# Another hand-written order of the attention phase on three engines of a two-block transformer kernel

## The chip, the cores and the metric

The kernel runs on one core of one Trainium2 chip. The metric is the device time of one execution in microseconds, lower is better. Of the kernel before there are three timed executions: 1290.80, 1287.97 and 1290.04 us, median 1290.04.

## The reference

256 rows of 1024 values pass through two layers of a first block and one layer of a second block, all in fp32. A layer of the first block, which the change touches, is:

```
h = rms_norm(x, attn_norm_g); z = h @ w_in
q, k of three kinds: rms_norm per head of 64, rotary tables
moba: 4 heads, causal softmax, values of 64
diff: 4 heads, softmax(q1 k1) - lam * softmax(q2 k2), values of 128, rms_norm, gain
dsa:  an indexer (8 heads: relu(q k), weighted sum) keeps the 64 best causal keys per row;
      4 heads attend to these alone
x = x + concat(moba, diff, dsa) @ w_out
h2 = rms_norm(x, ffn_norm_g)
x = x + (silu(h2 @ w_gate) * (h2 @ w_up)) @ w_down
```

## The kernel before, in words

The 256 rows are two row blocks r = 0, 1 of 128. Every large product is three matmuls: each fp32 operand is split into a high part and a low part, and high by high, high by low and low by high are summed in PSUM (lines 587 to 589). Weights come by DMA from SP's queue in chunks of 1 MB into a ring of three slots `raw`. ACT writes a chunk's high part (`split_hi`, in the attention phase called `hi(p, j)`, line 1227), DVE subtracts to get the low part (`split_lo`, `lo(p, j)`, line 1684), PE multiplies. ACT may write a slot's high part only when PE has used the chunk three before it; SP may load a slot when DVE is done with it.

Each engine (PE = TensorE, ACT = ScalarE, DVE = VectorE, POOL = GpSimd, SP = SyncE) runs its own program in the order in which it is written, and waits on semaphores. For the attention phase of each of the two layers the orders on PE, ACT and DVE are three long lists of calls, written out by hand; both layers use the same lists. Their parts are:

- `row_product(p, j, r)` on PE: product p (0 to 7, columns of `w_in`), half j of the depth, row block r. `copy_z(l, p, r)` on ACT moves the result from PSUM to `z`. (Below, a product half is one such call.)
- `square_heads`, `head_sums`, `scale_heads(l, s)`: ACT, DVE and ACT again form the per-head norm of head set s, 0 to 3. POOL rotates and scales the set (lines 510 to 522) and takes the norm from `scale_heads`. POOL works through the index heads first (line 517 ends them), then through the sets MQ, DQ, DK, SQ.
- `turn_heads(s, b)` on PE transposes a finished set (here s = 0 index heads, 1 index key, 2 MQ, 3 DQ, 4 DK, 5 SQ), `heads_copy` on ACT copies it to `headsT`. `index_key` on DVE rotates the index key.
- `index_scores`, `index_relu`, `index_sum`, `topk_rounds`, `topk_mask`: the indexer, on PE, ACT and DVE.
- For four groups of heads g = 0 to 3 (moba, diff, dsa, diff): `group_scores` on PE, `attend_mask` on DVE, `attend_exp` on ACT, for the diff groups `blend` on DVE (line 1865), `group_turn` on PE, `attend_copy` or `blend_copy` on ACT and DVE, `group_values` on PE; then `attend_out` on DVE, or `diff_stats` on ACT and `diff_norm` on DVE (lines 1885, 1890). All groups share the PSUM banks 2 to 4 for scores and bank 5 for values.
- `mix_turn` on PE turns the mixed rows, `turned_hi_copy` and `turned_lo_copy` split them, `out_product(n, j, r)` multiplies by `w_out`.
- POOL also subtracts for the chunks 18 and 20 of each layer (line 548); DVE passes these on by `lo_from_pool`.

Two waits tie the groups together and are quoted, for the scores and for the values:

```python
def attend_scores(A, q, k):
    eng.wait_ge(pT_act, 2 * A + 2)
    eng.wait_ge(pT_dve, A + 1)
...
def attend_values(A, v, dv):
    eng.wait_ge(pT_act, 2 * A + 4)
    eng.wait_ge(pT_dve, A + 2)
    eng.wait_ge(o_done, A + 2)
```

`A` counts groups over both layers. A group's scores thus wait until the turned probabilities of the group before are copied, and its values until the result of the group before has left bank 5.

## Time and profile before

| | |
|---|---|
| time, median of three | 1290.04 us |
| profiled execution, its own time | 1290.8 us |
| its span in the trace | 1289.0 us |
| PE busy | 1256.7 us, 97% |
| DVE busy | 823.2 us, 64% |
| ACT busy | 662.2 us, 51% |
| POOL busy | 184.3 us, 14% |
| chain that ended last | PE 82%, DVE 9%, issue 4%, ACT 3% |

The span is what the trace covers, the time also holds what lies around it. A busy share is an average over the whole program. In the chain of waits each moment of the span is put down to the engine that was waited for. The attention phase of layer 0 runs from 24 to 162 us of the span, that of layer 1 from 359 to 493 us. An idle time in brackets behind a row of the timeline is what the engine stood still just before the row, and what ended it.

### The profile page before, as it was taken

How to read it: one execution, taken by the hardware profiler on the slowest of the kernel's cores; microseconds unless marked ns; L12 is line 12 of the kernel's file. 1: busy time of each engine (PE TensorE's matmuls, PEld its weight loads, DVE VectorE, ACT ScalarE, POOL GpSimd, SP SyncE). 2: the span in 40 equal slices, each digit the busy share in tenths (PEclk: the TensorE clock that was granted, in tenths of full speed). 3: DMA queues.
4: the chain of work that ended last, by engine and by line, in shares of the span. 5: the costliest groups of instructions: out<-in, count | busy, mean ns of one | idle time of the engine just before them, and what ended most of it. 6: DMA issues, size and time to landing. Idle time of an engine off the chain costs nothing.

```text
span 1289.0 us, 16912 instructions
## 1 busy us (share of the span) xinstructions
PE 1256.7 (97%) x6430; PEld 1059.2 (82%) x6430; DVE 823.2 (64%) x983; ACT 662.2 (51%) x981; POOL 184.3 (14%) x162
## 2 busy tenths in 40 slices
PE   8999999999999999999999999999999999999998
PEld 6779788888887978888888899788997777888886
DVE  5898664455669876554457655866695676655444
ACT  5567454434564756344435544644547654634443
POOL 5863200000177620000000000000000003000000
PEclk9989999999999999999999998999999999999999
DMA  7424355556462434555564563343334355455551
GB/s 263 183 74 144 131 196 196 184 179 219 139 209 75 160 135 146 213 191 195 180 220 157 205 215 112 122 146 102 127 107 173 148 191 189 169 186 193 195 198 46
DMA packets 34219, 213.12 MB, mean 165 GB/s; under 512 B 4305, under 2 KB 5585, under 8 KB 11506
## 3 DMA queue, kind: packets, MB, share of 16 engines
q1 hardware_dynamic: 34098, 212.21, 46.6%
q8 instruction: 38, 0.62, 0.2%
q14 instruction: 19, 0.16, 0.0%
q0 software_dynamic: 64, 0.13, 0.0%
HBM read 211.28 MB, written 1.05 MB: 165 GB/s over the span
## 4 chain that ended last, share of the span: by engine, by line
PE 82%; DVE 9%; issue 4%; ACT 3%; DMA 1%; POOL 1%; POOLq 0%; DVEq 0%; ACTq 0%
PE bank L587 23%; PE bank L589 22%; PE bank L588 22%; PE bank L1001 3%; DVE wlo L1684 2%; PE bank L694 2%; PE bank L753 2%; ACT whi L1227 1%; DVE index L1778 1%; PE bank L841 1%; PE bank L713 1%; DMA raw<-in_w_values 1%; PE bank L615 1%; DVE z L2163 1%; PE bank L1111 1%
## 5 line engine op out<-in xcount | busy, mean ns | idle before, releaser
L1684 DVE TENSOR_TENSOR wlo<-raw,whi 128x2048 fp32r<-128x2048 f32 (+4 forms) x197 | 439.3, 2234 | 252.1 <-ACT whi L1227 250.6
L1227 ACT ACTIVATE whi<-raw 128x2048 fp32r<-128x2048 f32 (+5 forms) x201 | 369.3, 1843 | 133.9 <-PE bank L589 125.7
L587 PE MATMUL bank<-whi,hT_hi 128*128 128x512 f32 (+4 forms) x1040 | 408.2, 393 | 6.7 <-DVE wlo L1684 3.4
L589 PE MATMUL bank<-whi,hT_lo 128*128 128x512 f32 (+4 forms) x1040 | 399.4, 384 | 0.0
L588 PE MATMUL bank<-wlo,hT_hi 128*128 128x512 f32 (+4 forms) x1040 | 398.8, 383 | 0.0
L587 PEld LDWEIGHTS bank<-whi,hT_hi 128*128 128x128 f32 x1040 | 197.4, 190 | 46.7 <-issue 7.2
L589 PEld LDWEIGHTS bank<-whi,hT_lo 128*128 128x128 f32 x1040 | 196.9, 189 | 36.6
L588 PEld LDWEIGHTS bank<-wlo,hT_hi 128*128 128x128 f32 x1040 | 197.6, 190 | 33.3
L587 PE MATMUL bank<-whi,mixT_hi 128*128 128x512 f32 (+1 forms) x248 | 96.4, 389 | 6.5 <-DVE mixT_lo L1719 3.7
L589 PE MATMUL bank<-whi,mixT_lo 128*128 128x512 f32 (+1 forms) x248 | 94.5, 381 | 0.0
L588 PE MATMUL bank<-wlo,mixT_hi 128*128 128x512 f32 (+1 forms) x248 | 94.2, 380 | 0.0
L587 PE MATMUL bank<-whi,ffT_hi 128*128 128x512 f32 x240 | 93.7, 390 | 0.0
L589 PE MATMUL bank<-whi,ffT_lo 128*128 128x512 f32 x240 | 93.5, 390 | 0.0
L588 PE MATMUL bank<-wlo,ffT_hi 128*128 128x512 f32 x240 | 93.4, 389 | 0.0
L1350 ACT ACTIVATE sqr<-bank,ssq 128x256 f32<-128x256 f32 x66 | 31.1, 473 | 88.0 <-PE bank L589 88.0
L1359 ACT ACTIVATE ffT_hi<-bank 128x256 fp32r<-128x256 f32 x60 | 19.8, 382 | 101.1 <-PE bank L841 101.1
L587 PEld LDWEIGHTS bank<-whi,mixT_hi 128*128 128x128 f32 (+1 forms) x248 | 47.2, 190 | 16.5 <-issue 3.4
L1915 DVE SCALAR_TENSOR_TENSOR probs<-bank,ssq,sqr 128x256 f32<-128x256 f32 x66 | 31.4, 480 | 44.6 <-ACT sqr L1350 44.6
L589 PEld LDWEIGHTS bank<-whi,mixT_lo 128*128 128x128 f32 (+1 forms) x248 | 46.9, 189 | 8.9
L588 PEld LDWEIGHTS bank<-wlo,mixT_hi 128*128 128x128 f32 (+1 forms) x248 | 47.3, 191 | 8.2
L589 PEld LDWEIGHTS bank<-whi,ffT_lo 128*128 128x128 f32 x240 | 45.1, 188 | 9.4
L588 PEld LDWEIGHTS bank<-wlo,ffT_hi 128*128 128x128 f32 x240 | 45.1, 188 | 9.3
(284 smaller groups left out, 1463.6 us busy)
## 6 DMA issues: line engine op xcount, KB each, us to landing
raw<-in_ff_loop SPq DMA_DIRECT2D x90, 1024.0 KB, 4.8
raw<-in_w_groups SPq DMA_DIRECT2D x64, 1024.0 KB, 4.8
raw<-in_w_out SPq DMA_DIRECT2D x8, 1024.0 KB, 4.8
raw<-in_ff_first SPq DMA_DIRECT2D x6, 1024.0 KB, 4.8
raw<-in_w_values SPq DMA_DIRECT2D x8, 728.0 KB, 4.2
raw<-in_w_comp SPq DMA_DIRECT2D x4, 1024.0 KB, 6.5
raw<-in_ff_last SPq DMA_DIRECT2D x3, 1024.0 KB, 7.0
raw<-in_w_values SPq DMA_DIRECT2D x4, 736.0 KB, 7.0
```

What stands on the lines that cost most here:

```text
L587: eng.matmul(out, lhsT=hi, rhs=wh, start=start, stop=False)
L588: eng.matmul(out, lhsT=hi, rhs=wl, start=False, stop=False)
L589: return eng.matmul(out, lhsT=lo, rhs=wh, start=False, stop=stop)
L615: mm = eng.transpose(bank[6 + r][:, k * P:(k + 1) * P], src[:, r, c:c + P], ident[:, :])
L694: mm = eng.matmul(bank[2 + u][:, c:c + keys], lhsT=headsT[half, q(h), rows], rhs=headsT[half, k(h), 0:keys], start=True, stop=True)
L753: mm = eng.matmul(out, lhsT=probsT[:, r + kt, h * P:(h + 1) * P], rhs=v(kt, h), start=(kt == 0), stop=(kt == r))
L1001: mm = eng.matmul(out, lhsT=a[i % RING][:, w], rhs=hT[h][:, 4 * j + k, :], start=(j == 0 and k == 0 and n == 0 and c % 2 == 0), stop=(j == ...
L1227: eng.activation(whi[j][:, 0:n], raw[j][:, 0:n], ACT.Copy).then_inc(hi_ready, 1)
L1350: eng.activation(sqr[:, r * FF_STEP:(r + 1) * FF_STEP], out[r][:, 0:FF_STEP], ACT.Silu, scale=ssq[:, 4 + r:5 + r]).then_inc(silu_ready, 1)
L1359: eng.activation(dst[0][:, 0:2, r * P:(r + 1) * P], bank[6 + r][:, 0:2 * P].rearrange("p (k c) -> p k c", k=2), ACT.Copy).then_inc(ff_hi, 1)
L1684: eng.tensor_tensor(wlo[j][:, 0:n], raw[j][:, 0:n], whi[j][:, 0:n].bitcast(F32), ALU.subtract).then_inc(lo_ready, 1)
L1915: eng.scalar_tensor_tensor(out=probs[:, r, 0:FF_STEP], in0=out[r][:, FF_STEP:2 * FF_STEP], scalar=ssq[:, 4 + r:5 + r], in1=sqr[:, r * FF_S ...
```

## The change

The three lists are written in another order. No call is added or removed, apart from cuts: the tiles of `attend_exp(A + 0, ...)` are cut as (0, 1) and (2) instead of (0) and (1, 2), the three tiles of `attend_mask(A + 0, ...)` are one call again, and the selection rounds are cut as 0 to 1, 1 to 3, 3 to 4, 4 to 8. POOL's and SP's programs are the same. The diff is 100 lines of such lists; a few of them stand here:

```diff
@@ tensor @@
-                row_product(2, 0, 0); row_product(2, 0, 1); row_product(2, 1, 0); row_product(2, 1, 1)
-                turn_heads(0, 0); row_product(3, 0, 0); turn_heads(1, 0); row_product(3, 0, 1); turn_heads(0, 1)
+                row_product(2, 0, 0); row_product(2, 0, 1); turn_heads(0, 0); turn_heads(0, 1)
+                row_product(2, 1, 0); turn_heads(1, 0); row_product(2, 1, 1); index_scores(l, 0)
...
@@ scalar @@
-                hi(1, 0); copy_z(l, 0, 0); hi(1, 1); copy_z(l, 0, 1); hi(2, 0); lambda_exp(l); copy_z(l, 1, 0)
+                hi(1, 0); hi(1, 1); copy_z(l, 0, 0); copy_z(l, 0, 1); hi(2, 0); lambda_exp(l); hi(2, 1)
...
@@ vector @@
-                lo(1, 0); lo(1, 1); lambda_sums(l); lo(2, 0); lo(2, 1); lambda_value(l); lo(3, 0); lo(3, 1)
-                head_sums(l, 0, 0); index_key(l); head_sums(l, 0, 1); lo(4, 0); lo(4, 1); index_sum(l, 0)
+                lo(1, 0); lo(1, 1); lambda_sums(l); lo(2, 0); lo(2, 1); lambda_value(l); index_key(l); lo(3, 0)
+                lo(3, 1); head_sums(l, 0, 0); lo(4, 0); index_sum(l, 0); index_sum(l, 1); head_sums(l, 0, 1)
```

First place: ACT in layer 0, from the squares of the first head set to its scale (`hln`, `hrs` are the scale; `whi` 128x2048 a split of a chunk; `headsT` copies of turned heads). Before, the row of `hln` is followed by the split of chunk (4, 0):

```order
L1227 ACTIVATE whi<-raw 128x2048 x2
L1253 ACTIVATE z<-bank,ssq 128x512
L1267 ACTIVATE scr<-z 128x512
L1253 ACTIVATE z<-bank,ssq 128x512
L1267 ACTIVATE scr<-z 128x512
L1283 ACTIVATE headsT<-bank 128x512
L1272 ACTIVATE hln<-hss,eps 128x16
L1276 ACTIVATE hrs<-hln 128x16
L1227 ACTIVATE whi<-raw 128x2048
L1283 ACTIVATE headsT<-bank 128x256
L1227 ACTIVATE whi<-raw 128x2048
```

After (ACT's lines are higher by one there), where the first `whi` row is the split of (4, 0) and the second that of (4, 1):

```order
L1284 ACTIVATE headsT<-bank 128x512 x2
L1254 ACTIVATE z<-bank,ssq 128x512
L1268 ACTIVATE scr<-z 128x512
L1284 ACTIVATE headsT<-bank 128x256
L1228 ACTIVATE whi<-raw 128x2048
L1291 ACTIVATE probs<-bank 128x512 x2
L1254 ACTIVATE z<-bank,ssq 128x512
L1268 ACTIVATE scr<-z 128x512
L1228 ACTIVATE whi<-raw 128x2048
L1273 ACTIVATE hln<-hss,eps 128x16
L1277 ACTIVATE hrs<-hln 128x16
```

The scale stands behind the splits of (4, 0) and (4, 1), behind two rectified index scores (`probs`), and behind the copies of the turned index heads and key; before it stood ahead of both splits.

Second place: PE in layer 0, from the last transposes of group 2's probabilities (banks 3 and 4 from `probs`) on (`L615` turns mixed rows, `L694` scores, `L753` values of a plain group, `L720` and `L726` turn blended probabilities). Before:

```order
L713 MATMUL bank3<-ident,probs 128x128 x4
L713 MATMUL bank4<-ident,probs 128x128 x4
L615 MATMUL bank6<-ident,mix 128x128 x4
L615 MATMUL bank7<-ident,mix 128x128 x4
L694 MATMUL bank2<-headsT 128x128 x2
L694 MATMUL bank3<-headsT 128x256 x2
L694 MATMUL bank2<-headsT 128x128 x2
L694 MATMUL bank4<-headsT 128x256 x2
L753 MATMUL bank5<-z,probsT 128x64 x12
L587 MATMUL bank0<-whi2,mixT_hi 128x512
```

After:

```order
L713 MATMUL bank3<-ident,probs 128x128 x4
L713 MATMUL bank4<-ident,probs 128x128 x4
L694 MATMUL bank2<-headsT 128x128 x2
L694 MATMUL bank3<-headsT 128x256 x2
L694 MATMUL bank2<-headsT 128x128 x2
L694 MATMUL bank4<-headsT 128x256 x2
L753 MATMUL bank5<-z,probsT 128x64 x12
L615 MATMUL bank6<-ident,mix 128x128 x4
L615 MATMUL bank7<-ident,mix 128x128 x4
L720 MATMUL bank2<-ident,probs 128x128 x2
L726 MATMUL bank2<-ident,probs 128x128 x2
L726 MATMUL bank3<-ident,probs 128x128 x2
```

The two turns of the mixed rows have moved behind the scores and values, and the turn of group 3's blended probabilities, which came behind two out products (eight matmul triples), now follows at once; an out product half stands behind it.

Third place: DVE in layer 0, behind the mask of group 2 (`chosen` mask from `index`). Before:

```order
L1885 TENSOR_TENSOR dstat<-dstat,inv 128x4
L1890 SCALAR_TENSOR_TENSOR mix<-bank,dstat,sub_g 128x128 x4
L1684 TENSOR_TENSOR wlo<-raw,whi 128x2048
L1831 COPY probsT<-bank 128x512
L1719 TENSOR_TENSOR mixT_lo<-bank,mixT_hi 128x4x128 x2
L1822 TENSOR_TENSOR probs<-bank,causal 128x512
L1826 TENSOR_REDUCE nmax<-probs 128x4
L1819 TENSOR_TENSOR bank<-bank,causal 128x2x128
L1826 TENSOR_REDUCE nmax<-bank 128x2
L1819 TENSOR_TENSOR bank<-bank,causal 128x2x128
L1826 TENSOR_REDUCE nmax<-bank 128x2
```

After:

```order
L1831 COPY probsT<-bank 128x512
L1684 TENSOR_TENSOR wlo<-raw,whi 128x2048
L1885 TENSOR_TENSOR dstat<-dstat,inv 128x4
L1890 SCALAR_TENSOR_TENSOR mix<-bank,dstat,sub_g 128x128 x4
L1822 TENSOR_TENSOR probs<-bank,causal 128x512
L1826 TENSOR_REDUCE nmax<-probs 128x4
L1819 TENSOR_TENSOR bank<-bank,causal 128x2x128
L1826 TENSOR_REDUCE nmax<-bank 128x2
L1819 TENSOR_TENSOR bank<-bank,causal 128x2x128
L1826 TENSOR_REDUCE nmax<-bank 128x2
```

The scaling of group 1's result (L1885, L1890) has moved behind the copy of turned probabilities (L1831) and a subtraction, directly ahead of group 3's mask (L1822 on); the low part of the turned mix (L1719) has left the stretch. On ACT the statistics that L1885 waits for have moved in the same way, from ahead of group 2's exponentials to behind the copies of its turned probabilities.

## Rows read from the trace of the kernel before

**Rows 1.** Timeline, PE, layer 0: start us, us, operation, [idle before <- releaser].
```profile
46.88 0.44 PE L921 MATMUL bank<-ident,sqr 128*128 128x128 f32 x2 [0.73 <-DVE sqr L1744]
...
69.62 2.96 PE L694 MATMUL bank<-headsT 64*128 64x128 f32 x16 [1.50 <-ACT headsT L1283]
...
135.85 1.58 PE L739 MATMUL bank<-z,probsT 128*128 128x128 f32 x12 [0.72 <-DVE probsT L1878]
...
143.62 1.06 PE L615 MATMUL bank<-ident,mix 128*128 128x128 f32 x8 [0.73 <-issue]
...
145.75 0.47 PE L587 MATMUL bank<-whi,mixT_hi 128*128 128x512 f32 x1 [1.07 <-DVE mixT_lo L1719]
```

**Rows 2.** Timeline, PE, layer 1.
```profile
403.20 2.31 PE L694 MATMUL bank<-headsT 64*128 64x128 f32 x16 [1.36 <-ACT headsT L1283]
...
412.87 0.50 PE L587 MATMUL bank<-whi,hT_hi 128*128 128x512 f32 x1 [1.65 <-DVE wlo L1684]
```

**Rows 3.** Busy time by stretch: us, engines busy, PEclk (granted clock), DMA share.
```profile
70.00:78.00 8.00, 8.00 (x28) 6.04 (x27) 7.72 (x21) 1.32 (x1) 2.75 (x3) 0.57 0.00 0
...
146.00:150.00 4.00, 4.00 (x12) 3.09 (x12) 2.50 (x2) 1.17 (x1) 0.00 (x0) 0.57 0.73 262
...
404.00:412.00 8.00, 7.22 (x36) 5.48 (x34) 7.72 (x21) 2.93 (x5) 5.03 (x4) 1.00 0.00 0
```

**Rows 4.** Timeline, ACT, opening of layer 0.
```profile
22.23 0.69 ACT L1253 ACTIVATE z<-bank,ssq 128x512 f32<-128x512 f32 x1 [0.43 <-PE bank L589]
...
22.82 1.42 ACT L1227 ACTIVATE whi<-raw 128x1472 fp32r<-128x1472 f32 x1
```

**Rows 5.** Tile raw, stretch 10.5 to 14: the issue and its time to landing.
```profile
L361 SPq DMA_DIRECT2D raw<-in_w_values x1: 328/328/328, 12.2 to 12.2; - x1
...
DMA to landing us min/median/max: 9.9/9.9/9.9
```

**Rows 6.** Timeline, PE (two product halves, index scores) and POOL (first head set).
```profile
34.62 0.39 PE L587 MATMUL bank<-whi,hT_hi 128*128 128x512 f32 x1
...
37.34 0.39 PE L587 MATMUL bank<-whi,hT_hi 128*128 128x512 f32 x1
...
393.40 1.13 PE L678 MATMUL bank<-headsT 64*128 64x256 f32 x4
...
33.34 3.22 POOL L510 TENSOR_TENSOR gain<-z,rope_c 128x512 f32<-128x512 f32 x1
...
38.03 1.29 POOL L517 TENSOR_TENSOR z<-gain 128x512 f32<-128x512 f32 x1
```

**Rows 7.** Timeline, layer 1, POOL and DVE around set 2's rotation.
```profile
382.50 2.75 POOL L510 TENSOR_TENSOR gain<-z,gain_c 128x256 f32<-128x256 f32 x1
...
385.21 0.88 POOL L513 TENSOR_TENSOR gain<-z,gain_s 128x128 f32<-128x128 f32 x2
...
389.80 1.29 POOL L519 TENSOR_TENSOR gain<-gain 128x512 f32<-128x512 f32 x1
...
391.17 1.04 POOL L522 TENSOR_TENSOR z<-gain,hrs 128x512 f32<-128x512 f32 x1
...
382.36 2.29 DVE L1684 TENSOR_TENSOR wlo<-raw,whi 128x2048 fp32r<-128x2048 f32 x1 [2.44 <-ACT whi L1227]
```

**Rows 8.** Timeline, layer 1, ACT and DVE at the end of attention.
```profile
454.82 1.08 ACT L1315 ACTIVATE probsT<-bank 128x512 f32<-128x512 f32 x2
...
469.81 0.37 ACT L1328 ACTIVATE sqr<-bank,inv 128x128 f32<-128x128 f32 x1
...
457.78 0.69 DVE L1822 TENSOR_TENSOR probs<-bank,causal 128x512 f32<-128x512 f32 x1
...
463.38 1.53 DVE L1865 SCALAR_TENSOR_TENSOR probs<-probs,coef 128x128 f32<-128x128 f32 x4
...
471.92 2.72 DVE L1885 TENSOR_TENSOR dstat<-dstat,inv 128x4 f32<-128x4 f32 x1 [1.78 <-ACT dstat L1333]
...
474.67 1.13 DVE L1890 SCALAR_TENSOR_TENSOR mix<-bank,dstat,sub_g 128x128 f32<-128x128 f32 x4
```

More of the change, by code:

```diff
@@ new lines, in _ @@
+                group_scores(2); row_product(7, 1, 0); row_product(7, 1, 1); group_values(1); group_turn(2)
+                group_scores(3); group_values(2); mix_turn(0, 0); mix_turn(0, 1); group_turn(3)
+                out_product(0, 0, 0); group_values(3); out_product(0, 0, 1); out_product(1, 0, 0)
+                mix_turn(1, 0); mix_turn(1, 1); out_product(1, 0, 1); out_product(0, 1, 0); out_product(0, 1, 1)
+                out_product(1, 1, 0); turn_part(l * 3 + 2, 0, 0); turn_part(l * 3 + 2, 0, 1)
@@ L977, in _ @@
+                out_product(1, 1, 1)
                 three.act = hT
@@ new lines, in _ @@
+                hi(6, 0); copy_z(l, 4, 1); square_heads(l, 2, 1); attend_exp(A + 0, 0, (0, 1)); hi(6, 1)
+                scale_heads(l, 2); attend_exp(A + 0, 0, (2,)); heads_copy(l, 3, 0); copy_z(l, 5, 0)
+                attend_copy(A + 0, 0); square_heads(l, 3, 0); attend_copy(A + 0, 1); heads_copy(l, 3, 1)
+                hi(7, 0); copy_z(l, 5, 1); square_heads(l, 3, 1); heads_copy(l, 4, 0); heads_copy(l, 4, 1)
+                scale_heads(l, 3); attend_exp(A + 1, 1); copy_z(l, 6, 0); copy_z(l, 6, 1); hi(7, 1)
@@ new lines, in _ @@
+                split_hi(t0, 17); heads_copy(l, 5, 0); blend_copy(A + 1); heads_copy(l, 5, 1); split_hi(t0, 18)
+                attend_exp(A + 2, 0, in_bank=False); copy_z(l, 7, 0); split_hi(t0, 19); attend_copy(A + 2, 0)
+                attend_copy(A + 2, 1); diff_stats(l, 1); copy_z(l, 7, 1); attend_exp(A + 3, 1)
+                turned_hi_copy(l * 3 + 1, mixT, halves=(0,)); blend_copy(A + 3); diff_stats(l, 3)
+                split_hi(t0, 20); turned_hi_copy(l * 3 + 1, mixT, halves=(1,)); split_hi(t0, FFN1)
@@ L2034, in _ @@
-                topk_rounds(3, 4); attend_mask(A + 0, causal, (2,)); topk_rounds(4, 5); lo(6, 0)
-                topk_rounds(5, 6); lo(6, 1); head_sums(l, 3, 0); topk_rounds(6, 7); head_sums(l, 3, 1)
-                attend_copy(A + 0); lo(7, 0); attend_mask(A + 1, causal); attend_out(A + 0, 0, take(0))
-                blend(A + 1, 1); topk_rounds(7, 8); blend_copy(A + 1); topk_mask(); lo(7, 1)
-                attend_mask(A + 2, chosen); diff_norm(l, 1); mixed(1); split_lo(t0, 17); attend_copy(A + 2)
@@ L2039, in _ @@
-                turned_lo_copy(l * 3 + 1, mixT, halves=(0,)); attend_mask(A + 3, causal)
-                attend_out(A + 2, 0, take(2)); blend(A + 3, 1); blend_copy(A + 3); lo_from_pool(2 * l + 1)
-                split_lo(t0, 19); diff_norm(l, 3); mixed(3); turned_lo_copy(l * 3 + 1, mixT, halves=(1,))
-                lo_from_pool(2 * l + 2); split_lo(t0, FFN1); add_out(0, 0); add_out(0, 1); add_out(1, 0)
-                turned_lo_copy(l * 3 + 2, hT, halves=(0,)); add_out(1, 1); split_lo(t0, FFN1 + 1)
+                lo(1, 0); lo(1, 1); lambda_sums(l); lo(2, 0); lo(2, 1); lambda_value(l); index_key(l); lo(3, 0)
@@ new lines, in _ @@
+                lo(3, 1); head_sums(l, 0, 0); lo(4, 0); index_sum(l, 0); index_sum(l, 1); head_sums(l, 0, 1)
+                lo(4, 1); head_sums(l, 1, 0); lo(5, 0); index_sum(l, 2); index_sum(l, 3); index_sum(l, 4)
+                index_sum(l, 5); head_sums(l, 1, 1); topk_rounds(0, 1); lo(5, 1); topk_rounds(1, 3)
+                head_sums(l, 2, 0); attend_mask(A + 0, causal); head_sums(l, 2, 1); lo(6, 0); topk_rounds(3, 4)
+                lo(6, 1); attend_copy(A + 0); topk_rounds(4, 8); topk_mask(); attend_out(A + 0, 0, take(0))
@@ new lines, in _ @@
+                head_sums(l, 3, 0); head_sums(l, 3, 1); attend_mask(A + 1, causal); lo(7, 0); blend(A + 1, 1)
+                lo(7, 1); blend_copy(A + 1); split_lo(t0, 17); attend_mask(A + 2, chosen); attend_copy(A + 2)
+                lo_from_pool(2 * l + 1); split_lo(t0, 19); diff_norm(l, 1); mixed(1); attend_mask(A + 3, causal)
+                attend_out(A + 2, 0, take(2)); blend(A + 3, 1); turned_lo_copy(l * 3 + 1, mixT, halves=(0,))
+                blend_copy(A + 3); diff_norm(l, 3); mixed(3); turned_lo_copy(l * 3 + 1, mixT, halves=(1,))
@@ L2044, in _ @@
+                lo_from_pool(2 * l + 2); split_lo(t0, FFN1); add_out(0, 0); add_out(0, 1)
+                split_lo(t0, FFN1 + 1); turned_lo_copy(l * 3 + 2, hT, halves=(0,)); add_out(1, 0); add_out(1, 1)
                 turned_lo_copy(l * 3 + 2, hT, halves=(1,))
```

49 lines of the change are left out of this document (15 added, 34 removed).

## The prediction

> **What bounds the kernel now.** The table of the page comes first: TensorE (PE) is busy 97% of a span of 1289.0 us, and the chain that ended last is 82% PE. A new order can therefore change the time only by what PE waits for, and by its clock. Second come PE's own rows in time order, which carry in brackets how long it stood idle and for whom. Between two blocks of matmuls it stands still at five places of layer 0's attention: 0.73 us for the index key, 1.50 us for the turned heads that the first group's scores read, 0.72 us for a copy of turned probabilities, and 0.73 and 1.07 us around the turn of the mixed rows: 4.75 us [rows 1]. Layer 1 has no wait for the key; it waits 1.36 us at the first scores and 1.65 us for the low part of the first weight chunk of product 5 [rows 2], and the last three again as in layer 0: 5.53 us. Together 10.3 us. Third, the granted clock: behind the 1.50 us wait the stretch 70 to 78 runs at 0.57, behind the pair 0.73 and 1.07 the stretch 146 to 150 does too, both a mix of the two levels 2.4 and 1.2 GHz; behind layer 1's 1.36 us wait 404 to 412 stays at 1.00 [rows 3]. At 0.57 the lost work is 8 x 0.43 = 3.4 us and 4 x 0.43 = 1.7 us, 5.2 us in all. So at most 15.5 us of this region are waits and clock; the rest is matmuls that the change neither adds nor removes. Below, (p,j,r) is product p, half j, row block r. The part behind the last out product is left alone.
>
> **The change part by part.** No instruction is added or dropped; only what stands ahead of what on PE, ACT and DVE. POOL and SP keep their programs, but are released at other moments.
>
> **What it takes away.** The key's rotation stands ahead of the splits on DVE, and its turn comes one half product later: the 0.73 us go. The low part of product 5's chunk is written before index sums 2 to 5 instead of behind three selection rounds: the 1.65 us go. The heads of set 2 are copied ahead of the next split: 1.50 and 1.36 us go. At the end, an out product half now follows the last turn of the mixed rows and covers its copies, and the split of chunk 20 stands behind the statistics, so that POOL's subtraction doesn't run against the scaling (it stretched the small operation at 471.92 to 2.72 [rows 8]): with the copy's 0.72 all three late waits go in both layers. What is late next is worked out now.
>
> **Opening, layer 0 only.** The copy of z that frees the bank for product 1 starts at 22.23 and takes 0.69; it now stands behind the next split, whose data were issued at 12.2 and landed 9.9 us later, at 22.1. The split takes 1.42, so the copy starts at 23.5, 1.3 us later [rows 4, 5]. The subtraction for the product's own chunk, which also gates it and ends last today, covers a part of this; of 0 to 1.3 us I take 0.55.
>
> **First head turn, layer 0 only.** PE ends (2,0,1) at 37.34, with the opening's delay at 37.9; there it now wants set 0 turned, one and a half products earlier than before. POOL rotates that set until 38.03 + 1.29 = 39.3 [rows 6], so at least 1.4 us are waited. Its operation of 1.3 us takes 3.22 at 33.34 where a DVE subtraction runs beside it [rows 6]. The key's four operations and the split of chunk (3,0) now fall into the second row block's rotation; a whole subtraction in front would put it at about 41.5 (3.6 us), the short ones alone at 40.3. I take the latter, near to the row: 2.4 us. In layer 1 POOL doesn't have to build its tables ahead of this set, and I count no wait.
>
> **Set 2 (the MQ rows), both layers.** This is the reason in the first half. Count from the end of (3,0,1). ACT's split of (4,1) waits for that chunk and takes 2.0; only behind it stands the scale, ready at 2.55. DVE's subtraction runs 2.0 to 4.25, and POOL, which would multiply, is held until then: in the trace one half-wide operation takes 2.75 beside a 2.29 us subtraction that began 0.14 earlier, while two of the next kind take 0.88 together [rows 7]. So the multiply (1.04) ends at 5.3. The second row block has 3.3 of rotation (two pairs of 0.88 and two single operations of about 0.75), then 1.29 and 1.04 [rows 7], with gaps 5.8; the subtraction of (5,0), 7.5 to 9.7, holds it 2.2 us again: 13.3. PE gets there after three half products of 2.72 [rows 6] and three index scores of about 1.1 [rows 6]: 11.5. It waits 1.85 us (0.8 without the second hold, 2.8 with a third). In the kernel before the scale stood ahead of the split of (4,0) and this set was ready in time.
>
> **Set 4 (the DK rows), both layers.** POOL carries that lateness on: from 13.3 the third set ends at about 28.5, the fourth, held twice by the 1456 wide subtractions, at 42.4, where PE wants it at 41.4: 1.0 us (0 to 1.5), an estimate from the same rows. Group 2's scores wait another 0.3 for a head copy behind two splits.
>
> **The end of attention, both layers, the largest term.** Between turning group 2's probabilities and scoring group 3 PE now has nothing, where it had the turn of the mixed rows; the score writes banks that ACT must first copy. The two copies take 1.08 [rows 8], and the split of chunk 19 (1.9) stands ahead of them: 0.75 to 2.7 us, I take 1.1, since the selected mask leaves ACT late and PE too. Call the end of the copies C. Scores end at C + 2.3. But the statistics of group 1 now stand behind these copies: 469.81 to 471.9 for the like of them, then the scaling on DVE, 1.13 and a small operation ahead of it [rows 8], so DVE begins group 3's mask at C + 3.4, and group 2's values wait for the same scaling since they share a bank. From the mask's start to the end of the blend it is 457.78 to 463.38 + 1.53 = 7.1 us [rows 8]: the blend ends at C + 10.5. PE has values (2.75), two turns (0.85) and half of its own turn between, and would be there at C + 6.4: 4.2 us waited. The low copies of the turned mix come behind the blend on DVE and cost 0.3 more. 5.6 us a layer; the 4.2 are firm, since nothing in that chain overlaps (3.2 to 5).
>
> **The sum.** Layer 0: 0.55 + 2.4 + 1.85 + 1.0 + 0.3 + 5.6 = 11.7. Layer 1: 1.85 + 1.0 + 0.3 + 5.6 = 8.75. Added 20.45, removed 10.3: +10.15. The two slow stretches of today go with their waits: -5.2, to +5.0. New waits bring new ones. I take one behind the first head turn (2.4) and one behind each tail (more than 4 us within 7): three at the mean of the two shown, 2.6: +7.7. In all +12.7 us on the profiled execution's 1290.8: 1303.5. That execution is 0.8 above the median of the runs, 1290.04, so on the median's scale 1302.7.
> The Trainium skill, TensorE: Matmul & The Clock Gate, section "HAM oscillation — how this bites in real kernels", has a matmul kernel in which every wait for data is followed by a cold start, without exception, at 1.67 us of throttling each, half of it lost. This trace is milder in how often (1.36 and 1.65 us cost no clock) and harsher in price (3.4 and 1.7); by the page's figure the three would be 2.5 us, an estimate, and the time 1297.5.
>
> **Rivals.**
> A. The clock holds. The waits are as above and cost only themselves: +5.0, 1295. For it: layer 1's two waits of like length, both at 1.00. Against it: the new waits are longer than any here. Chance 0.15.
> B. Every wait over 1.5 us drops the clock: both set 2 waits too, five stretches of 3.4 us: 5.0 + 17.2 = +22.2, 1312. This is the way the skill's page just named has it (each wait pays). For it the row behind 1.50 us; against it the rows of layer 1. Chance 0.10.
> C. POOL is held less than I count, because its operations slip between DVE's: first turn 1.4, set 2 0.8, set 4 nothing: 5.1 us less, and two stretches: 5.0 - 5.1 + 5.2 = +5.1, 1295. For it: with two subtractions in a row POOL does get an operation in between. Against: each row of it beside a subtraction is 2 us long. Chance 0.20.
> D. The other side: the tail's chain is not late. If group 1's statistics and scaling ran beside the scores, so that the blend ended 4.1 us behind them, the 4.5 us a layer vanish; with set 2 waits too short for the clock that is 5.0 - 9.0 = -4.0, 1286. It decides at 4.1 us from the end of scores 3 to the end of the blend; today mask to blend alone are 7.1 [rows 8]. Chance 0.08.
> That the new order leaves the work in place as if unchanged (waits traded one for one) has 0.02. The forecast itself has 0.45.
>
> **How the numbers follow.** Forecast 1302.7, its own spread 1297 to 1309 from the bounds of set 2, set 4 and the copies. The range goes down over A and C with their spread to 1292.5, and up to 1311, which leaves out D and most of B. A difference under 0.2%, about 2.6 us, can't be told from none. Faster holds most of D and nothing else: 0.06; same 0.04; slower 0.90.
>
> **What would show it.** In the changed profile PE's rows should have idle brackets at: the first turn of layer 0 for POOL's z, near 38, above 1.4 us; the turn of set 2 in both layers for POOL's z, near 2 us, with the wait at the first scores and the one for product 5's chunk gone; the scores of group 3 for ACT's copies; the values of group 2 and the turn of group 3 for DVE, together 4 us or more; and none at the turn of the mixed rows of half 1. The granted clock should fall below 1 behind the tail's wait in both layers. Blend minus scores under 5 us would break the largest term; a clock of 1.00 in all new stretches would make it A.

## The result and the profile after

The changed kernel takes 1300.15 us (median of four, 1299.77 to 1301.81); in the same comparison the kernel before took 1289.43. The ratio is 1.0086, 95% interval 1.0068 to 1.0103: slower by 0.9%. Run a second time beside the last experiment it took 1300.35, ratio 1.0095 (1.0079 to 1.0110). The prediction was 1302.7, 12.7 us over before; measured are 10.7 and, the second time, 12.0. The profiled execution took 1302.03, against 1290.80 before. One execution each of two kernels further down (2530.68 and 3218.31 us) was disturbed and is left out.

The page of the profile after, its span, its busy table and the chain that ended last:

```profile
span 1300.2 us, 16907 instructions
PE 1265.1 (97%) x6430; PEld 1065.9 (82%) x6430; DVE 813.7 (63%) x983; ACT 663.7 (51%) x981; POOL 181.9 (14%) x162
PE 76%; DVE 8%; POOL 7%; issue 4%; ACT 3%; DMA 1%; SPq 0%; POOLq 0%; DVEq 0%; ACTq 0%
```

PE is busy 8.4 us longer for the same 6430 matmuls, so its clock was lower somewhere (the mean granted clock of the span is 0.982, before 0.990), and POOL, which held 1% of the chain before, holds 7%. Both point to the same places in PE's rows. Its timeline of layer 0, idle time in brackets (ACT's line numbers are one higher than before):

```profile
39.08 1.09 PE L921 MATMUL bank<-ident,z 128*128 128x128 f32 x8 [0.86 <-POOL z L517]
...
66.43 1.11 PE L921 MATMUL bank<-ident,z 128*128 128x128 f32 x4 [3.11 <-POOL z L522]
...
98.39 0.88 PE L921 MATMUL bank<-ident,z 128*128 128x128 f32 x6 [0.26 <-POOL z L522]
...
126.01 2.31 PE L694 MATMUL bank<-headsT 64*128 64x128 f32 x16 [1.10 <-ACT probsT L1316]
129.21 3.81 PE L753 MATMUL bank<-z,probsT 128*128 128x64 f32 x24 [0.89 <-DVE mix L1890]
135.57 0.69 PE L720 MATMUL bank<-ident,probs 128*128 128x128 f32 x2 [0.84 <-DVE probs L1865]
```

The five waits of [rows 1] are gone and these have come: first head turn, set 2, set 4, scores of group 3, values of group 2, turn of group 3. In layer 1 the two of [rows 2] are gone, there is none at the first head turn, and the other five are the same within 0.02 us:

```profile
404.34 1.11 PE L921 MATMUL bank<-ident,z 128*128 128x128 f32 x4 [3.11 <-POOL z L522]
...
436.30 0.88 PE L921 MATMUL bank<-ident,z 128*128 128x128 f32 x6 [0.26 <-POOL z L522]
...
463.90 2.31 PE L694 MATMUL bank<-headsT 64*128 64x128 f32 x16 [1.10 <-ACT probsT L1316]
467.11 3.79 PE L753 MATMUL bank<-z,probsT 128*128 128x64 f32 x24 [0.90 <-DVE mix L1890]
473.44 0.69 PE L720 MATMUL bank<-ident,probs 128*128 128x128 f32 x2 [0.82 <-DVE probs L1865]
```

The slow stretches of [rows 3] at 70 and 146 are gone as well; new ones stand behind the 3.11 us wait and at the tail, in both layers (busy time by stretch, the granted clock is the third number from the right):

```profile
66.00:70.00 4.00, 3.57 (x11) 2.40 (x12) 2.85 (x3) 1.01 (x2) 3.84 (x5) 0.51 0.12 48
70.00:74.00 4.00, 4.00 (x14) 3.26 (x13) 3.16 (x10) 0.78 (x2) 0.85 (x1) 0.64 0.01 2
...
132.00:136.00 4.00, 3.16 (x15) 2.62 (x14) 3.34 (x11) 3.32 (x13) 0.00 (x0) 0.50 0.02 6
136.00:140.00 4.00, 3.90 (x13) 3.07 (x12) 1.93 (x4) 0.60 (x1) 0.00 (x0) 0.50 0.00 0
...
404.00:408.00 4.00, 3.66 (x11) 2.49 (x12) 2.78 (x3) 1.11 (x2) 3.84 (x5) 0.50 0.06 23
408.00:412.00 4.00, 4.00 (x15) 3.21 (x13) 3.67 (x10) 0.69 (x2) 0.79 (x1) 0.65 0.01 2
...
468.00:472.00 4.00, 4.00 (x25) 4.00 (x25) 3.58 (x8) 3.35 (x16) 0.00 (x0) 0.60 0.48 199
472.00:476.00 4.00, 3.07 (x12) 2.08 (x11) 3.54 (x9) 1.79 (x5) 0.00 (x0) 0.50 0.01 2
476.00:480.00 4.00, 4.00 (x14) 3.21 (x13) 0.00 (x0) 0.00 (x0) 0.00 (x0) 0.62 0.00 0
```

Clock 0.50 is the 1.2 GHz level throughout; the other numbers mix it with 2.4 GHz. Behind each 3.11 us wait 8 us run at 0.5 to 0.65: 4 x 0.49 + 4 x 0.36 = 3.4 us of work lost. At the tail the clock falls earlier than at the last wait: in layer 0 at about 131.0, in the middle of group 2's values, when PE had waited 1.10 and 0.89 us; it is back at about 141.

Where the time went, by PE's starts: layer 1's attention begins 4.8 us later than before (363.55 against 358.72), layer 1's feed-forward part 11.9 us later (501.91 against 490.01), and the whole span is 11.2 longer; block two gives 0.7 back. By the first matmul of group 1's turn the changed kernel had lost 1.9 us in layer 0 (111.81 against 109.87) and 2.6 more in layer 1, so the head costs 4.6 us and the tail 2.9 + 4.4 = 7.3 us.

### The profile page after: what moved, and what is told of

The parts are those of the page before. It is cut to its first block, busy times and chain, and to the rows that moved or that the text cites. A ratio compares the mean times of both kernels' runs of the same rounds, so it can differ in the third digit from the quotient of the medians.

```text
span 1300.2 us, 16907 instructions
## 1 busy us (share of the span) xinstructions
PE 1265.1 (97%) x6430; PEld 1065.9 (82%) x6430; DVE 813.7 (63%) x983; ACT 663.7 (51%) x981; POOL 181.9 (14%) x162
## 4 chain that ended last, share of the span: by engine, by line
PE 76%; DVE 8%; POOL 7%; issue 4%; ACT 3%; DMA 1%; SPq 0%; POOLq 0%; DVEq 0%; ACTq 0%
PE bank L587 21%; PE bank L589 21%; PE bank L588 21%; PE bank L1002 3%; DVE wlo L1684 2%; POOL gain L513 2%; POOL z L522 2%; PE bank L694 2%; PE bank L753 1%; ACT whi L1228 1%; PE bank L841 1%; POOL gain L510 1%; ACT probs L1305 1%; DMA lam_c<-in_lam_init 1%; PE bank L713 1%
```

## The experiments

Each kernel was timed on the same chip as the kernel before, and a ratio is to that; the kernel before took 1288.46 us beside the first four, 1288.11 beside the 22 transposes, the first two pieces of the tail and the first list from both, 1286.89 beside the third piece and the second list, and 1288.32 beside the kernel with both causes undone and the changed kernel again. Across these groups ratios are compared.

**The head alone.** The changed lists up to product (7,0,0) on PE (the scale of set 3 on ACT, the blend of group 1 on DVE), before's lists behind that.

```diff
 ... row_product(6, 1, 1); row_product(7, 0, 0); group_turn(1); turn_heads(5, 0); turn_heads(5, 1)
-row_product(7, 0, 1); group_scores(2); row_product(7, 1, 0); row_product(7, 1, 1); group_values(1) ...
+group_values(1); group_scores(2); row_product(7, 0, 1); row_product(7, 1, 0); row_product(7, 1, 1) ...
```

> The changed lists up to product (7,0,0) on PE, the scale of set 3 on ACT and the blend of group 1 on DVE; behind that the lists of before. If costs add by place: up to the turn of group 1 the changed kernel had lost 1.9 us in layer 0 and 2.6 in layer 1, so the time is 1289.4 + 4.6 = 1294.0, with the 3.1 us wait for set 2 and the slow stretch behind it in both layers, and no slow clock at group 3. Rival, all of the loss is in the tail (the head only shifts waits that the tail gives back): 1289 to 1291. Rival, the two halves depend on each other (a tail made for the other head): over 1297.

1296.51 us, ratio 1.0069 (1.0056 to 1.0082), 8.0 us over before and 2.5 over what was expected. The 3.11 us waits and the slow clock behind them are there, the tail has neither the changed kernel's waits nor its slow clock. 2.9 of the 8.0 us are of the seam: ACT, in this mixture, copies product (6,0) only after an exponential, and PE waits in both layers, here in layer 0:

```profile
111.71 0.41 PE L587 MATMUL bank<-whi,hT_hi 128*128 128x364 f32 x1 [1.47 <-ACT z L1253]
```

Without it the head costs 5.1 us, near the 4.6 read by place.

**The tail alone.** The same cut the other way round: the lists of before, and behind the cut the changed ones.

> The lists of before up to the same points, behind them the changed ones. If costs add by place: the changed kernel lost 2.9 us behind the turn of group 1 in layer 0 and 4.4 in layer 1, block two gave 0.7 back, so 1289.4 + 7.3 - 0.7 = 1296.0, with the waits of 1.1 and 0.9 us at groups 3 and 2 and the slow clock behind them. Rival, the tail waits are there only because the changed head delivers later: 1289 to 1292. Rival, the halves depend on each other: over 1299.

1294.98 us, ratio 1.0054 (1.0041 to 1.0067), 6.5 us over before, where 6.6 was expected. The tail's waits do not need the changed head: they are there with the old one. Head 5.1 and tail 6.5 make 11.6, the changed kernel's loss (10.7 and 12.0 in its two comparisons): the halves add, if the 2.9 us of the seam are taken at their face.

**The scale early.** In the changed kernel the second row block's copy and square go ahead of the split of (4,0), the scale goes between the splits of (4,0) and (4,1), ahead of two rectified scores, and DVE sums the squares ahead of its split of (4,0).

```diff
@@ scalar @@
-hi(4, 0); index_relu(l, 0); index_relu(l, 1); copy_z(l, 2, 1); square_heads(l, 0, 1); hi(4, 1); scale_heads(l, 0)
+copy_z(l, 2, 1); square_heads(l, 0, 1); hi(4, 0); scale_heads(l, 0); index_relu(l, 0); index_relu(l, 1); hi(4, 1)
@@ vector @@
-lo(4, 0); index_sum(l, 0); index_sum(l, 1); head_sums(l, 0, 1)
+head_sums(l, 0, 1); lo(4, 0); index_sum(l, 0); index_sum(l, 1)
```

> The changed kernel with one thing moved back: the copy and the square of row block 1 of product 2 and the scale of set 0 stand ahead of the split of (4,1) and the rectified scores, and DVE sums the squares ahead of the low split of (4,0). If the 3.1 us waits for set 2 come from the late scale and the slow clock from the waits, both go in both layers: 1300.2 - 2 x (3.1 + 3.4) = 1287.2. Rival, the wait goes and the clock falls there anyway: 1300.2 - 6.2 = 1294. Rival, POOL's multiply and PE meet another late part (the index scores or the set after it) as soon as this one is early: 1291 to 1297, with a new wait of 1 to 2 us before 100 us of the span.

1292.22 us, ratio 1.0031 (1.0019 to 1.0042). Set 2 is turned without a wait, and the clock stays up:

```profile
63.96 0.66 PE L921 MATMUL bank<-ident,z 128*128 128x128 f32 x4
```
```profile
64.00:68.00 4.00, 4.00 (x22) 3.11 (x22) 3.88 (x5) 2.36 (x5) 3.10 (x3) 1.00 0.64 224
68.00:72.00 4.00, 4.00 (x24) 3.04 (x23) 3.77 (x9) 2.33 (x3) 0.39 (x1) 1.00 0.01 2
```

The cause is right, the size is not: some 8 us came back (7 to 8 by the ratios), not 13. The last rival named the reason, a next late part, and its 1291 to 1297 hold the time, but the part stands at another place than it said: PE, by group 3's scores now 4.4 us earlier in layer 0 and 8.7 in layer 1, waits for the blend of group 1, 0.67 us in layer 0 and 1.46 in layer 1, because, as the order reads, the changed list does four selection rounds ahead of it (the lists further down move rounds behind it, and the wait is gone); and the tail's wait ahead of L720 is 2.6 us in layer 1. The clock still falls at the tail, for some 10 us in layer 0.

```profile
107.71 0.66 PE L726 MATMUL bank<-ident,probs 128*128 128x128 f32 x4 [0.67 <-DVE probs L1865]
```
```profile
441.42 0.66 PE L726 MATMUL bank<-ident,probs 128*128 128x128 f32 x4 [1.46 <-DVE probs L1865]
```

**The wait without the slow clock.** PE transposes the identity into the free bank 6 while it would stand still; nothing reads it.

```diff
+def filler(s, count):
+    eng.wait_ge(heads_copied[0], turned_sets(l, s, 0))
+    for q in range(count):
+        eng.transpose(bank[6][:, 0:P], ident[:, :], ident[:, :])
...
-index_scores(l, 4); turn_heads(2, 0)
+index_scores(l, 4); filler(2, 10); turn_heads(2, 0)
```

> The changed kernel with ten transposes of the identity into bank 6 ahead of the first transposes of set 2, in the 3.1 us in which PE stands still; nothing reads what they write. The set comes no earlier, so the wait's 3.1 us stay spent. If the slow clock behind it is a price of its own on top of the wait: 1300.2 - 2 x 3.4 = 1293.4, granted clock 1.00 between 66 and 74 us. Rival, the clock drop costs nothing further (PE would only have waited for ACT or DVE later): 1300. Rival, the clock falls in spite of the filler: 1300 or a little more, clock 0.5 there.

1299.79 us, ratio 1.0095 (1.0080 to 1.0109), but the runs don't agree: the profiled execution took 1295.62, the others 1299.06 to 1301.19. In the profiled one ten transposes filled 1.3 us, 1.87 were left, and the clock stayed at 1.00 behind them. No trace of the others says where, but their mean granted clock was lower: 0.986 at 1300.53, 0.987 at 1301.19 and 0.991 at 1299.06, against 0.994 in the profiled one. So the same kernel was run with 22.

> The changed kernel with 22 transposes of the identity ahead of the first transposes of set 2 instead of ten: ten took 1.3 us and left 1.9 us of the wait, so 22 fill 2.9 of the 3.1 us; nothing reads them. With ten the clock stayed at 1.00 in the profiled execution (1295.6) but the timed runs of that kernel lay between 1295.6 and 1301.2. If the slow clock is a price of its own that follows from PE standing still: the clock stays up in every execution, 1300.2 - 2 x 2.5 = 1295.2 (with ten, the turn of group 1 came 2.4 to 2.5 us earlier in each layer), runs close together. Rival, the clock's fall is not tied to this wait: runs spread as with ten, median 1299 or more.

1295.97 us, ratio 1.0061 (1.0047 to 1.0075), all five runs between 1295.17 and 1296.40, with a mean granted clock of 0.990 to 0.993 where the changed kernel had 0.982 to 0.986. PE, and the stretches behind:

```profile
63.48 2.62 PE L958 MATMUL bank<-ident 128*128 128x128 f32 x22
66.68 0.66 PE L921 MATMUL bank<-ident,z 128*128 128x128 f32 x4 [0.57 <-POOL z L522]
```
```profile
66.00:70.00 4.00, 3.43 (x19) 2.55 (x19) 3.58 (x4) 1.78 (x3) 3.84 (x5) 1.00 0.13 54
70.00:74.00 4.00, 4.00 (x25) 3.03 (x23) 3.86 (x10) 2.13 (x3) 1.22 (x1) 1.00 0.03 6
```

Set 2 is turned no sooner, and the kernel is 3 to 4 us faster by its ratio. The slow clock is thus a price of its own, a little smaller than the 5.0 us expected. In the profile the turn of group 1 comes 2.5 us earlier in each layer, counted from the first head turn, though 3.4 us of work had been lost: set 4 is waited for 0.69 us instead of 0.26, which is half of the 0.9 between them.

**The chain at the tail, one piece.** DVE's low split of chunk 19 goes behind the copy of group 3's probabilities.

```diff
@@ vector @@
-lo_from_pool(2 * l + 1); split_lo(t0, 19); diff_norm(l, 1) ... blend_copy(A + 3); diff_norm(l, 3)
+lo_from_pool(2 * l + 1); diff_norm(l, 1) ... blend_copy(A + 3); split_lo(t0, 19); diff_norm(l, 3)
```

> The changed kernel with one DVE call moved back: the low split of chunk 19 stands behind DVE's copy of group 3's turned probabilities instead of ahead of the masks of group 3. The split took 2.3 us on DVE between the copy for group 2's values and the masks of group 3. If the turn of group 3 is late by the chain scores, masks, exponentials, blend, and this split is in the chain: masks up to 2.3 us earlier, the wait ahead of L720 (2.6 us at full clock) down to about 0.3, so 1300.2 - 2 x 2.3 = 1295.6. Rival, ACT's statistics and DVE's norm of group 1 hold the masks anyway: masks earlier by under 0.5 us, 1299 to 1300. Rival, the split is late for the out products at its new place: a new wait at L587 after the mixed rows' turn, over 1300.

1300.72 us, ratio 1.0091 (1.0075 to 1.0106): nothing gained; the first rival named the mechanism, its time (1299 to 1300) is 0.7 short. The profiled execution, 1305.11, was the slowest of its four. DVE now stands idle where the split was, and the norm starts when ACT's statistics are done:

```profile
129.96 0.16 DVE L1885 TENSOR_TENSOR dstat<-dstat,inv 128x4 f32<-128x4 f32 x1 [2.10 <-ACT dstat L1334]
130.16 1.13 DVE L1890 SCALAR_TENSOR_TENSOR mix<-bank,dstat,sub_g 128x128 f32<-128x128 f32 x4
131.46 0.69 DVE L1822 TENSOR_TENSOR probs<-bank,causal 128x512 f32<-128x512 f32 x1 [0.18 <-DVE mix L1890]
```

From the scores of group 3 to its turn it is 9.57 us, where the changed kernel has 9.56 (126.01 to 135.57).

**A second piece.** ACT's high split of chunk 19 moved too.

```diff
@@ scalar @@
-attend_exp(A + 2, 0, in_bank=False); copy_z(l, 7, 0); split_hi(t0, 19); attend_copy(A + 2, 0) ... blend_copy(A + 3)
+attend_exp(A + 2, 0, in_bank=False); copy_z(l, 7, 0); attend_copy(A + 2, 0) ... blend_copy(A + 3); split_hi(t0, 19)
```

> As the kernel before this one, and ACT's high split of chunk 19 moved too, behind ACT's copy of group 3's turned probabilities. It stood ahead of the copies of group 2's turned probabilities, which came 1.1 us after PE was done. If it holds the copies and, behind them, the statistics of group 1: the 1.1 us wait ahead of group 3's scores falls to 0.3, the norm comes 1.9 us earlier, the masks and the turn of group 3 with them: a further 0.8 to 1.9 us per layer, so 1292 to 1294. Rival, the wait goes but the turn of group 3 stays where it is: 1295 to 1296, with a longer wait ahead of L720.

1302.16 us, ratio 1.0109 (1.0094 to 1.0125); the profiled execution, 1297.57, was its fastest (mean granted clock 0.989, the others 0.984 and 0.985). The wait at the scores fell by 0.2 only, since DVE's own copy ends it; the one at the values fell from 0.9 to 0.5, and ahead of L720 stood

```profile
134.35 0.44 PE L720 MATMUL bank<-ident,probs 128*128 128x128 f32 x2 [2.58 <-DVE probs L1865]
```

That the turn of group 3 stays nearly where it was is the rival's mechanism, but its time, 1295 to 1296, is as wrong as the expected 1292 to 1294. The row also shows what a slow clock hides: at this tail the clock was 1.00, behind the wait too, up to 160 us of the span, and the wait 2.58; in the changed kernel they were 0.50 and 0.84. The distance from scores to turn is 9.17 against 9.56. In layer 1 the same wait, also 2.58, came with a clock of 0.50 from 468 to 474.

**A third piece.** Group 1's values, statistics and norm in addition, which is close to where before had them. (The minus lines are those of the second piece.)

```diff
@@ tensor @@
-row_product(7, 0, 1); group_scores(2); row_product(7, 1, 0); row_product(7, 1, 1); group_values(1); group_turn(2)
+row_product(7, 0, 1); group_values(1); group_scores(2); row_product(7, 1, 0); row_product(7, 1, 1); group_turn(2)
@@ scalar @@
-split_hi(t0, 18); attend_exp(A + 2, 0, in_bank=False) ... attend_copy(A + 2, 1); diff_stats(l, 1)
+split_hi(t0, 18); diff_stats(l, 1); attend_exp(A + 2, 0, in_bank=False) ... attend_copy(A + 2, 1)
@@ vector @@
-attend_mask(A + 2, chosen); attend_copy(A + 2); lo_from_pool(2 * l + 1); diff_norm(l, 1); mixed(1)
+attend_mask(A + 2, chosen); diff_norm(l, 1); mixed(1); attend_copy(A + 2); lo_from_pool(2 * l + 1)
```

> The kernel with both splits of chunk 19 moved, and in addition the values of group 1 back ahead of group 2's scores on PE, their statistics on ACT and their norm on DVE with them. With the splits alone the masks of group 3 still stood behind the norm of group 1 on DVE, and the norm behind ACT's statistics, which waited for the late values: from group 3's scores to its turn it was 9.2 to 9.6 us in every variant of the changed tail at full clock. If the late values of group 1 are what holds this chain: the wait of 0.5 us ahead of group 2's values goes, the masks start 1 us after the scores instead of 3.3, the turn of group 3 comes 7.3 us behind its scores, the wait ahead of L720 is about 1.2 us instead of 2.6: 2.3 us per layer less than the changed kernel's 1300.2, 1295.7, a little less if the clock stays up there. Rival, the exponentials and the blend alone fill 9 us: L720 where it was, 1300. Rival, PE is held at the new place of the values by the copies of group 1 (over 0.5 us at L739): 1297 to 1299.

1297.76 us, ratio 1.0080 (1.0065 to 1.0095), 2.1 over the expectation. The number lies in the range of the last rival, but not for its reason: PE doesn't wait at the values' new place. The interval overlaps those of the changed kernel, so the gain, 0.8 to 1.9 us by the ratios, is hardly clear of noise; the rows carry the argument. The wait at group 2's values is gone, DVE is idle ahead of the masks until the scores are there, and

```profile
128.05 0.69 DVE L1822 TENSOR_TENSOR probs<-bank,causal 128x512 f32<-128x512 f32 x1 [1.76 <-PE bank L694]
```
```profile
134.34 0.44 PE L720 MATMUL bank<-ident,probs 128*128 128x128 f32 x2 [1.89 <-DVE probs L1865]
```

The distance fell to 7.91 us: 1.6 from the scores' start to the masks, 6.3 to the turn. So values, statistics and norm of group 1 together are what held the masks, and the splits were in their shadow; the three were not moved one by one, nor without the splits. But 7.9 us of masks, exponentials and blend stand against some 6 us of PE work (scores, values, two mix turns), and a wait of 1.9 stays. Before had two halves of the out product there too. From group 1's turn to the last turn of mixed rows in layer 1 it is 54.95 us in the changed kernel, 54.77 with the two splits moved, 52.23 here, 50.51 before. In layer 0 it is 54.97, 52.38, 52.50 and 52.09, with the clock at 1.00 in the second only.

**Both causes undone.** The early scale and the third piece together.

> The changed kernel with both of its named causes undone: the scale of set 0 early, as measured before by itself (3.8 us over before), and the values, statistics and norm of group 1 with both splits of chunk 19 as in the kernel that moved all of them. In that kernel the stretch from the turn of group 1 to the last turn of mixed rows took 52.2 to 52.5 us against 55.0 in the changed kernel and 52.1 or 50.5 in the kernel before. If the loss is these two things and they add: before + 3.8 - 2 x 2.6 = before - 1.4, with the late blend of group 1 (0.7 and 1.5 us) still in it. Rival, the early head makes other parts late (the blend, group 2's masks), so that the tail's gain is lost again: before + 2 to + 4.

1287.55 us, ratio 0.9992 (0.9983 to 1.0001), 0.8 us under before, expected 1.4 under. The changed kernel beside it took 1300.35, so the two things named are worth 12.8 us together, and without them the new order is level with the old one. That is a balance, not a kernel without waits: in its profile PE waits 10.4 us at seven places (1.93 at the first head turn, then per layer some 1.5 for the blend of group 1, 0.88 at the scores of group 3 and 1.89 ahead of L720), as much as the 10.3 that the change took away. Alone the scale was worth 8 us and the tail's pieces 2 or less; beside the early scale the same pieces are worth 5 (1292.22 to 1287.55). Why it is more than the sum wasn't settled. Part of it is clock: the executions' mean granted clock is 0.983 to 0.986 in the changed kernel beside it, 0.986 to 0.990 with the tail's pieces alone, 0.989 to 0.992 with the early scale alone and 0.991 to 0.994 with both.

**A list from both.** The changed head with the early scale, the index head turns behind half (2,1,0), the opening of before, two of the selection rounds behind the blend; before's tail, with the statistics of group 3 ahead of the split of chunk 20 and half (1,0,1) of the out product behind the last mix turn.

> A list put together from both: the changed head with the scale of set 0 early, the two index head turns behind product half (2,1,0), the last two selection rounds behind the blend of group 1, before's order from the copies of group 1 on, but the statistics of group 3 ahead of the high split of chunk 20 and half (1,0,1) of the out product behind the last mix turn; the opening as before. If costs add by place: the changed kernel with the early scale measured 3.8 us over before; its tail cost 6.5 us, its late blend 2.1, its first head turn and opening 1.5 in layer 0, and the last mix turn gives 1.0 in each layer: before + 3.8 - 6.5 - 2.1 - 1.5 - 2.0 = before - 8.3, about 1280. Rival, a seam between the two halves costs again (the copies of the last z product were 1.5 us late when before's tail stood behind the changed head): 1283 to 1287. Rival, nothing is left because DVE and POOL exclude each other elsewhere: 1288 or more.

1287.36 us, ratio 0.9992 (0.9982 to 1.0003), with runs from 1283.02 to 1290.49: no faster, where about 1280 was expected. The fast ones had a mean granted clock of 0.995, the slowest 0.989. PE waited 1.88 us in each layer for DVE's copy behind the two rounds:

```profile
108.85 0.35 PE L739 MATMUL bank<-z,probsT 128*128 128x128 f32 x1 [1.88 <-DVE probsT L1876]
```

So one round was moved behind that copy, and ACT's last exponential of group 0 and the scale of set 2 ahead of a split:

```diff
@@ scalar @@
-attend_exp(A + 0, 0, (0, 1)); hi(6, 1); scale_heads(l, 2); attend_exp(A + 0, 0, (2,))
+attend_exp(A + 0, 0, (0, 1)); attend_exp(A + 0, 0, (2,)); scale_heads(l, 2); hi(6, 1)
@@ vector @@
-blend(A + 1, 1); topk_rounds(6, 8); blend_copy(A + 1); topk_mask()
+blend(A + 1, 1); topk_rounds(6, 7); blend_copy(A + 1); topk_rounds(7, 8); topk_mask()
```

> The list put together from both, with two waits of its own taken out: DVE copies group 1's turned probabilities after one selection round instead of two (PE waited 1.9 us for that copy in each layer), and ACT's last exponential of group 0 and the scale of set 2 stand ahead of the high split of (6,1) (0.8 us at L713 in layer 0, 0.6 us for set 4 in layer 1). If these waits were paid in full: 1287.4 - 2 x 1.4 - 0.8 - 0.6 = 1283.2, and the runs lie closer together than 1283.0 to 1290.5, since no wait over 1 us is left in the attention phase. Rival, the waits move to the masks of group 2 or the chunk of product 6: 1286 to 1287. Rival, the spread came from block two: 1283 with the same spread.

1280.29 us, ratio 0.9948 (0.9935 to 0.9962): 0.5% faster than the kernel before, the fastest of all (five runs from 1279.73 to 1280.86) and better than expected: 1283.2 stood against 1287.4 for the list before it, a gain of 4.2. Between the two profiled executions, both at clock 1.00 in the attention phases, 3.5 us went, of which PE's waits in these phases explain 2.2; the medians differ by some 6 us by their ratios. The rest of that is clock: the runs of the first list had a mean granted clock of 0.989 to 0.995, with 0.992 in the middle, these 0.995 and 0.996. No wait over 0.91 us is left in the attention phases, and the spread is gone.

**The changed kernel again**, without an edit, on the chip of the kernel with both causes undone.

> The changed kernel as it is, a second time, for a comparison on the same chip as the kernel with both causes undone, and for the spread of its runs: the variants with only splits or values moved lay between 1297.6 and 1305.1, one of them with the 0.9 and 2.6 us waits of the tail in another stage of the clock. Expected 1299 to 1301, before + 10.7 to + 12, with 3.1 us waits for set 2 in both layers. If the clock falls by chance, its profile may show other slow stretches at the tail than the first one, with the wait ahead of L720 between 0.8 (slow clock ahead of it) and 2.6 (full clock): the sum of both nearly the same.

1300.35 us, four runs from 1299.93 to 1302.74, 12.0 over before. The waits for set 2 are 3.11 us again. The one ahead of L720 reads 1.36 us in layer 0, where values of group 2 took 3.29 us instead of 3.81:

```profile
129.85 3.29 PE L753 MATMUL bank<-z,probsT 128*128 128x64 f32 x24 [0.90 <-DVE mix L1890]
136.21 0.69 PE L720 MATMUL bank<-ident,probs 128*128 128x128 f32 x2 [1.36 <-DVE probs L1865]
```

The two sums, 4.65 and 4.65, are equal: what the clock takes, the wait gives back.

## Why the prediction was right

The time, 1300.15, lies 2.6 us under the forecast, and the two largest reasons, the late scale and the late chain at the tail, were there. That the number is so near is partly luck: the size of most terms was off, in both directions, and so were the places of the slow clock. By its steps:

- **The waits removed** (10.3 us) and the slow stretches of before (5.2 us): all gone as named.
- **Opening**, 0.55: product (1,0,0) starts at 24.37, before at 23.65: 0.72.
- **First head turn**, 2.4: measured 0.86. This step failed. The key's four DVE operations do fall into POOL's rotation, but POOL ended at 39.03, no later than before; the short ones cost it nothing to be seen, and the split of (3,0) began after it. It lies below the lower bound of 1.4, which took POOL's old end and PE's new start at 37.9; PE ended at 38.2. The wait isn't the same in every execution: two of the ten profiles with this opening show 1.93 and 1.97 us, nearer to the forecast.
- **Set 2**, 1.85: measured 3.11 in both layers, and the mechanism is there row by row. DVE's subtractions and the POOL operations beside them:

```profile
55.29 2.29 DVE L1684 TENSOR_TENSOR wlo<-raw,whi 128x2048 fp32r<-128x2048 f32 x1 [1.14 <-ACT whi L1228]
...
60.73 2.29 DVE L1684 TENSOR_TENSOR wlo<-raw,whi 128x2048 fp32r<-128x2048 f32 x1 [2.55 <-ACT whi L1228]
```
```profile
55.84 2.64 POOL L522 TENSOR_TENSOR z<-gain,hrs 128x512 f32<-128x512 f32 x1 [7.47 <-ACT hrs L1277]
...
60.79 3.01 POOL L513 TENSOR_TENSOR gain<-z,gain_s 128x128 f32<-128x128 f32 x2
```

  Counted from the end of (3,0,1) at 53.34, POOL is done at 66.37, 13.0 us where 13.3 was forecast. The size was off on PE's side: it got there after 10.0 us instead of 11.5. The three index scores took 2.0 us together. The forecast had 1.1 each from one row of [rows 6], whose length holds the modelled end of a pipelined matmul; such rows overlap when they follow each other, and only the distance of their starts may be added.
- **Set 4**, 1.0: 0.26. The lateness was shorter in part because PE itself came later, by its slow clock: with the clock up, behind the 22 transposes, it is 0.69. **Group 2's scores**, 0.3: no wait.
- **The tail**, 5.6 a layer: 1.10 at the scores (forecast 1.1). The copies ended at 125.75 and the blend at 136.30, 10.5 us later, as forecast. At full clock the waits behind are 0.90, 2.61 and 0.35 (with 22 transposes at the head), 3.9 us where 4.2 stood; with the slow clock 0.89 and 0.84. The low copies' 0.3 wasn't seen. The experiments confirm the cause, statistics and norm of group 1 behind the late values, and show that the splits alone are not it.
- **The clock**, three stretches at 2.6 = 7.7: the number is close, the places are not. None lies behind the first head turn (0.86 us), one lies behind each set 2, and the one at each tail begins before the long wait, not behind it. A stretch at set 2 costs 2.5 us in the end. At the tail 5.1 us of clock are lost in layer 0, but most of it runs while PE would wait anyway. From group 1's turn to the last mix turn it takes 54.97 us, against 52.38 with the two splits moved and the clock up; 0.6 of the difference is the splits', so the slow clock costs 2.0. The second run of the changed kernel shows the same without another kernel: in its layer 1 the slow stretch, 470 to 474, ended before the turn at 474.53 and cost nothing behind it, and the distance is 52.96 (450.78 to 503.74), 2.0 less. Two at 2.5 and two at about 2 make 9, though 17 us of work were lost.

The sum with measured terms: waits 0.72 + 0.86 + 2 x (3.11 + 0.26 + 5.0) = 18.3 against 20.45, clock 9 against 7.7; 18.3 + 9 - 10.3 - 5.2 = 11.8 where 11.9 was measured at the end of layer 1. By place the same terms give 1.8 and 2.9 for the heads of layer 0 and 1 and 2.8 and 4.5 for their tails, where 1.9, 2.6, 2.9 and 4.4 were read. Against the forecast set 2 and the clock came out 2.5 and 1.3 us larger, the first turn, set 4, group 2's scores and the tail 4.8 smaller; these errors cancelled in part.

**The rivals.** A (the clock holds) is what the 22 transposes made of the head alone. B (every wait over 1.5 us drops it) fits set 2, and the work lost in all, 17.0 us, is close to its 17.2; but lost work isn't time: 3.4 us of it cost 2.5 at set 2, and 5.1 about 2 at the tail. Its rule fails too. The clock fell at the tail when no single wait had been over 1.10 us, and a wait over 1.5 us did not always drop it: 1.88 us twice in one profile, 1.93 once and 2.58 once cost no clock. The kernel with DVE's one split moved shows that one such wait can, at the place where the prediction had it (the clock is 0.50 from 41 to 44):

```profile
39.67 1.09 PE L921 MATMUL bank<-ident,z 128*128 128x128 f32 x8 [1.97 <-POOL z L517]
```

The Trainium skill, TensorE: Matmul & The Clock Gate, section "HAM oscillation — how this bites in real kernels", has the clock fall at every one of a kernel's waits for data, which last some 3 to 5 us there. The traces agree for the waits of 3.11 us: in both layers of every profile that has one unfilled, the clock fell behind it. Of shorter waits the kernel in the Trainium skill shows nothing. Here 0.86 us at the first head turn left the clock at 1.00, and of the waits of 1.4 to 2.6 us some did and some did not; what decides it no run here shows. C (POOL is held less) was nearer for the first turn and set 4 and wrong for set 2. D (the tail is not late) would have had the blend end within 4.1 us of the end of the scores; it ended 8.0 us behind it (128.3 to 136.30).

## What to carry to other kernels

When an order is changed, work out for each engine's queue what now stands ahead of the one operation that another engine waits for: here one scale behind one 1.9 us split, and one block of values placed late with its statistics and norm, make up the whole difference to before. A chain held by several operations in parallel gives nothing back when one of them is moved (the split of chunk 19); look for the call that makes the others late, here the values. And when the clock falls behind a wait, count that too: 3.11 us of waiting cost some 2.5 us more. But don't add lost work as if it were time where a longer wait follows, since slow work runs in its shadow. One profile shows one execution; where executions differ by some us, compare their mean granted clocks before explaining the profile.

## What the runs showed that was not expected

- Ten transposes into an idle gap of 3.1 us held the clock in the profiled execution; the others, at a lower mean clock (0.986 to 0.991), took some 5 us longer. With 22 all five were close together. Work that computes nothing made the kernel 3 to 4 us faster.
- What a profile shows for one wait depends on the clock around it: the same wait ahead of L720 reads 0.84, 0.94, 1.36 and 2.6 us in kernels with the same tail, and the row is ended by the same blend each time.
- Waits of 1.88 us in each layer left the clock at 1.00 in the profiled execution, yet taking them out, with some smaller waits, brought the median 6 us and the executions within 1.2 us of each other. The other executions of the kernel with these waits had a mean clock down to 0.989; that it fell behind these waits is likely, but no trace of them shows the place.
